# Expert weights of 64 tokens: five spread units on TensorE and 128 accumulating transfers by GpSimd in place of six units

## The reference, cut to what matters

```python
q = (hb @ w_q).reshape(n, PEER_HEADS, 2, PEER_HALF)            # 8 heads, 2 sides: 16 "sides" of 128
s = jnp.einsum('nhid,hikd->nhik', q, sub_keys)                 # 128 scores for each side
s_top, i_top = lax.top_k(s, PEER_TOPK)                         # 16 of 128 for each side
cand = s_top[:, :, 0, :, None] + s_top[:, :, 1, None, :]
best, pos = lax.top_k(cand.reshape(n, PEER_HEADS, 256), PEER_TOPK)
idx = take_along_axis(cand_idx, pos)                           # one of 16384 experts = 128 x 128
w = jax.nn.softmax(best, axis=-1)
act = jax.nn.gelu(einsum('nhkd,nd->nhk', u_tab[idx], hb))
out = einsum('nhk,nhkd->nd', w * act, v_tab[idx])
```

## Time and profile before

| | |
|---|---|
| median of 3 runs | 2785.63 us |
| the profiled execution's own time | 2787.02 us |
| its span | 2785.2 us |
| TensorE busy | 2717.4 us |
| VectorE, ScalarE, GpSimd busy | 1929.9, 1030.8, 621.7 us |
| query stage | about 855 to 949 us |
| pass over U | about 953 to 1606 us |
| pass over V | about 1610 to 2130 us |

### The profile page before, as it was taken

How to read it: one execution, slowest core, us unless ns; L and a number is a source line. 1 busy time by engine, 2 the same in 40 slices (tenths; PEclk the granted TensorE clock), 3 DMA queues, 4 the chain that set the end, 5 groups by cost and what they waited for, 6 DMA issues and landing times. The chain is left out here.

```text
span 2785.2 us, 41401 instructions
## 1 busy us (share of the span) xinstructions
PE 2717.4 (98%) x15226; PEld 2352.7 (84%) x15226; DVE 1929.9 (69%) x3331; ACT 1030.8 (37%) x1505; POOL 621.7 (22%) x436
## 2 busy tenths in 40 slices
PE   8999999999999999999999999999999999999998
PEld 7887788898887898999999988888887777788887
DVE  7676563434545579999968778888888655588843
ACT  6433343223333343444444333333334434332222
POOL 4333100000000166566664322222220000100000
PEclk9999999999999999999999999999999999999999
DMA  3111222211223267899999999999996211223332
GB/s 131 46 54 54 76 96 79 82 39 61 94 96 106 91 198 260 252 292 293 292 285 353 363 323 345 346 346 348 343 345 216 64 51 61 68 99 99 99 89 78
DMA packets 254581, 488.27 MB, mean 175 GB/s; under 512 B 102737, under 2 KB 160209, under 8 KB 253666
## 3 DMA queue, kind: packets, MB, share of 16 engines
q1 hardware_dynamic: 199138, 326.88, 35.8%
q0 software_dynamic: 36864, 134.23, 13.2%
q10 hardware_dynamic: 18432, 25.17, 2.6%
HBM read 437.97 MB, written 48.23 MB: 175 GB/s over the span
## 5 line engine op out<-in xcount | busy, mean ns | idle before, releaser
L285 PE MATMUL banks<-weights_high,experts_third 128*128 128x512 f32 x768 | 298.8, 389 | 1.0 <-DVE experts_third L2335 1.0
L287 PE MATMUL banks<-weights_high,experts_third 128*128 128x512 f32 x768 | 298.8, 389 | 0.0
L286 PE MATMUL banks<-weights_low,experts_third 128*128 128x512 f32 x768 | 298.8, 389 | 0.0
L2146 POOL TENSOR_TENSOR weights_low<-weights_raw,weights_high 128x1024 fp32r<-128x1024 f32 x66 | 158.2, 2396 | 468.8 <-ACT weights_high L2045 468.6
L285 PE MATMUL banks<-hn_high,weights_high 128*128 128x264 f32 (+1 forms) x736 | 253.5, 344 | 4.4 <-DVEq L2698 1.7
L2102 ACT ACTIVATE weights_high<-weights_raw 128x1024 fp32r<-128x1024 f32 x128 | 135.8, 1061 | 328.7 <-PE banks L287 328.7
L285 PE MATMUL banks<-hb_high,weights_high 128*128 128x384 f32 x688 | 238.1, 346 | 9.2 <-POOL weights_low L2146 9.2
L286 PE MATMUL banks<-hn_low,weights_high 128*128 128x264 f32 (+1 forms) x736 | 246.8, 335 | 0.0
L287 PE MATMUL banks<-hn_high,weights_low 128*128 128x264 f32 (+1 forms) x736 | 245.6, 334 | 0.0
L287 PE MATMUL banks<-hb_high,weights_low 128*128 128x384 f32 x688 | 231.3, 336 | 0.0
L286 PE MATMUL banks<-hb_low,weights_high 128*128 128x384 f32 x688 | 231.2, 336 | 0.0
(11 more groups left out here) (579 smaller groups left out, 7084.3 us busy)
## 6 DMA issues: line engine op xcount, KB each, us to landing
weights_raw<-in_u SPq DMA_DIRECT2D x128, 512.0 KB, 3.4
weights_raw<-in_v SPq DMA_DIRECT2D x128, 512.0 KB
early_experts<-experts_A ACTq DMA_DIRECT2D x128, 192.0 KB
shared<-early_experts SPq DMA_DIRECT2D x128, 192.0 KB
weights_raw<-in_w_up SPq DMA_DIRECT2D x44, 512.0 KB, 3.4
expert_weights<-shared SPq DMA_DIRECT2D x40, 512.0 KB
shared<-expert_weights SPq DMA_DIRECT2D x128, 160.0 KB
weights_raw<-in_w_xbc SPq DMA_DIRECT2D x24, 512.0 KB, 3.4
```

What stands on the lines that cost most here:

```text
L285: nc.tensor.matmul(to, w[0], x[0], start=start, stop=False)
L286: nc.tensor.matmul(to, w[0], x[1], start=False, stop=False)
L287: return nc.tensor.matmul(to, w[1], x[0], start=False, stop=stop)
L2146: nc.gpsimd.tensor_tensor(u_places[t % 3][1], raw[:, t % RING, :], u_places[t % 3][0].bitcast(F32), ALU.subtract).then_inc(u_low, 1)
```

## The change

- The first unit (tokens 128 to 191) isn't spread. Its 64 x 128 weights are added to the table in HBM by 128 indirect transfers of GpSimd, one per choice, each with 64 partitions and 4 bytes a partition, with add as the operation. Every 16 of them wait until the earlier ones have landed, since two heads may choose one expert. Their columns of the table are zeroed in the query stage by 8 stores of SP.
- Five units are spread, at the tiles of the new `SPREAD_AT`; block 1 has one unit, blocks 2 and 3 have two. Four are stored.
- Twelve of the 16 sides are scored by PE in the middle of query tiles 3 to 14 and copied back by ScalarE; of these VectorE ranks sides 0 to 11 of block 0 and 6 to 11 of block 1 in the query stage, 18 rows. The other four sides are scored before tile 0 for all blocks; the tables follow tile 0.
- Two `settle()` of `route_choice` take dots. `EXP_AT`, `DOT_AT` and `GATHER_AT` are some 3 or 4 tiles earlier. Low parts go to VectorE from tile 96 on instead of 100.

```diff
+RANKED_EARLY = (tuple(range(0, 12)), tuple(range(6, 12)), (), ())
+SIDES_EARLY = 12
-EXP_AT = (13, 27, 50, 76)
-SPREAD_AT = [start + min(i // 3, 4) for start in (30, 42, 56, 68, 83, 95) for i in range(HALF // PER)]
+EXP_AT = (10, 24, 45, 71)
+SCATTERED = HALF
+FIRST_SPREAD = 1
+SPREAD_AT = [start + at for start in (27, 52, 64, 79, 91) for at, n in enumerate((3, 3, 3, 3, 4)) for i in range(n)]
+SCATTER_AT = [t for t in range(28, 126) for _ in range(2 if t > 95 else 2 if t in SPREAD_AT else t % 2)]
+SCATTER_AT = SCATTER_AT[:P]
+ZERO_PARTS = 8
...
 GATHER_AT = (
-    39, 41, 42, 43, 44, 44, 44, 45, 45, 45, 46, 46, 47, 52, 53, 54, 56, 57, 58, 58, 58, 59, 59, 59,
+    37, 39, 40, 41, 42, 42, 42, 43, 43, 43, 43, 43, 44, 49, 49, 50, 52, 53, 54, 54, 54, 55, 55, 55,
...
# queries_phase, SP
+                    if m - RING < ZERO_PARTS:
+                        sp.dma_start(w_dram[(m - RING) * rows:(m - RING + 1) * rows, :, 0:SCATTERED].rearrange("i j n -> j i n"),
+                                     zeros[:].unsqueeze(1).to_broadcast([P, rows, SCATTERED])).then_inc(zeroed, 16)
...
+                sp.wait_ge(zeroed, 16 * ZERO_PARTS)
# queries_phase, PE
+                def score(r):
+                    if r == 0:
+                        pe.wait_ge(*keys_loaded)
+                    pe.wait_ge(evicted, r + 1)
+                    if r >= 2:
+                        pe.wait_ge(scores_out, r - 1)
+                    for b in range(NB):
+                        last = nc.tensor.matmul(B[:, SCORES + r % 2, b * P:(b + 1) * P], q[:, b, r, :], keys[:, r, :], start=True, stop=True)
+                    last.then_inc(scored, 1)
...
+                        if c == 3 and 0 <= m - 3 < SIDES_EARLY:
+                            score(m - 3)
# queries_phase, VectorE, once for each of the five ranking steps, around evict, normed and hb_low
+                    for b in rows:
+                        rank(nc.vector.max(top[b][:, r, 0:8], q[:, b, r, :]))
                     evict(m - 2)
+                    ranked()
...
# experts_phase, SP before the pass over V
-                sp.wait_ge(w_stored, 16 * STORES * (HALVES - 1))
+                sp.wait_ge(w_stored, 16 * STORES * (SPREAD_HALVES - 1))
+                sp.wait_ge(scattered, 16 * P)
# experts_phase, GpSimd
+                def scatter(g):
+                    if g == 0:
+                        pool.wait_ge(row_index, 7)
+                    elif g % TOPK == 0:
+                        pool.wait_ge(scattered, 16 * g)
+                    nc.gpsimd.indirect_dma_start(table, bass.IndirectOffsetOnAxis(ap=place[0:SCATTERED, g:g + 1], axis=0),
+                                                 place_w[0:SCATTERED, g:g + 1], None, compute_op=ALU.add).then_inc(scattered, 16)
...
+                    for n in scatters_after(t):
+                        scatter(n)
                     for g in gathers_after(t):
# experts_phase, VectorE after route_choice(1)
+                    if b == 1:
+                        settle()
+                        nc.vector.scalar_tensor_tensor(row_f[:], picked[:, 0, :], float(KEYS), picked[:, 1, :], ALU.mult, ALU.add
+                                                       ).then_inc(row_index, 1)
+                        nc.vector.tensor_copy(place_w[:], picked[:, 2, :]).then_inc(row_index, 1)
+                        dve.wait_ge(row_index, 6)
+                        nc.vector.tensor_scalar(place[:], row_f[:], float(STORED), column[:, 0:1], ALU.mult, ALU.add).then_inc(row_index, 1)
                     dve.wait_ge(chosen_out, b)
```

More of the change, by code:

```diff
@@ L1579, in _ @@
                 add_skip(G - 1, NB - 1)
[L1582 removed]
+RANKED_EARLY = (tuple(range(0, 12)), tuple(range(6, 12)), (), ())
+SIDES_EARLY = 12
+EARLY_STEPS = 5 * sum(len(r) for r in RANKED_EARLY)
+ROWS_LEFT = [[r for r in range(2 * PEER_HEADS) if r not in early] for early in RANKED_EARLY]
+STEPS_TO = [EARLY_STEPS + sum(5 * (len(ROWS_LEFT[i]) + PEER_HEADS) + 25 for i in range(b)) for b in range(NB + 1)]
 HALF = 64
 PER = 4
+LOW = -3.0e38
 DENSE = SEQ - P
 STORED = DENSE - HALF
[L1587 to L1588 removed]
+EXP_AT = (10, 24, 45, 71)
[5 more added lines that the diff above has]
+ZERO_PARTS = 8
 TAIL = SPREAD_AT[-1] + 1
@@ L1643, in _ @@
             def _(sp):
+                sp.wait_ge(constants_set, 1)
                 for m in range(RING, TILES):
@@ L1762, in _ @@
                         k.split_low(dve)
+                    r = m - 5
+                    rows = [b for b in range(NB) if r in RANKED_EARLY[b]]
+                    if rows:
+                        dve.wait_ge(scores_out, r + 1)
+                    for b in rows:
+                        rank(nc.vector.max(top[b][:, r, 0:8], q[:, b, r, :]))
                     evict(m - 2)
+                    ranked()
+                    for b in rows:
+                        rank(nc.vector.max_index(idx[b][:, r, 0:8], top[b][:, r, 0:8], q[:, b, r, :]))
                     if 4 <= m < 4 + KD:
@@ L1767, in _ @@
                                                        ).then_inc(scaled, 1)
+                    ranked()
+                    for b in rows:
+                        rank(nc.vector.match_replace(q[:, b, r, :], top[b][:, r, 0:8], q[:, b, r, :], LOW))
                     if 6 <= m < 6 + KD:
@@ L1773, in _ @@
                                                 ).then_inc(hb_low, 1)
+                    ranked()
+                    for b in rows:
+                        rank(nc.vector.max(top[b][:, r, 8:16], q[:, b, r, :]))
+                    ranked()
+                    for b in rows:
+                        rank(nc.vector.max_index(idx[b][:, r, 8:16], top[b][:, r, 8:16], q[:, b, r, :]))
+                assert done[0] == EARLY_STEPS
 def begin_load_phase(k, name, pairs):
@@ L1789, in gathers_after, with scatters_after @@
     return [g for g in range(P) if GATHER_AT[g] == t]
+def scatters_after(t):
+    return [n for n in range(len(SCATTER_AT)) if SCATTER_AT[n] == t]
 def slot_uses(g):
@@ L1799, in spread_groups, with spread_from, experts_phase @@
     return [n for n in range(len(SPREAD_AT)) if SPREAD_AT[n] == t]
+def spread_from(b):
+    return max(0, 2 * (b - 1) - FIRST_SPREAD) * (HALF // PER)
 def block_begun(t):
     groups = spread_groups(t)
-    return groups[0] // (HALF // PER * 2) + 1 if groups and groups[0] % (HALF // PER * 2) == 0 else 0
-def experts_phase(k, name, following, q, out, keys, hb, u, v, u_rows, by_token, gathered, early, w_dram, ws, es, keys_loaded):
+    return {spread_from(b): b for b in range(1, NB)}.get(groups[0], 0) if groups else 0
+def experts_phase(k, name, following, q, out, keys, hb, u, v, u_rows, by_token, gathered, early, w_dram, ws, es, ranks, tops, idxs):
     nc = k.nc
@@ L1895, in _ @@
                         sp.dma_start(raw[:, t % RING, :], u[t]).then_inc(raw_in[t % RING], 16)
-                    for half in range(HALVES - 1):
+                    for half in range(SPREAD_HALVES - 1):
                         last = SPREAD_AT[(half + 1) * GROUPS - 1]
@@ L1927, in _, with score_rest @@
             def _(pe):
-                def score(b):
-                    if b:
-                        pe.wait_ge(scores_out, b)
-                    for r in range(SIDES):
-                        last = nc.tensor.matmul(B[:, 2 + r // 4, (r % 4) * KEYS:(r % 4 + 1) * KEYS], q[:, b, r, :],
-                                                keys[:, r, :], start=True, stop=True)
+                def score_rest():
+                    for r in range(SIDES_EARLY, SIDES):
+                        for b in range(NB):
+                            last = nc.tensor.matmul(B[:, 2 + r - SIDES_EARLY, b * P:(b + 1) * P], q[:, b, r, :], keys[:, r, :],
+                                                    start=True, stop=True)
                     last.then_inc(scored, 1)
@@ L2274, in one_hots @@
                         dve.wait_ge(spread_done, n - 1)
-                    four = slice(n * PER, (n + 1) * PER)
-                    here = (n * PER) % P
+                    four = slice(column_of(n), column_of(n) + PER)
+                    here = column_of(n) % P
                     pairs = [P, 2, PER, P]
@@ L2291, in _ @@
                 nc.vector.tensor_copy(row_i[:], row_f[:]).then_inc(row_index, 1)
+                nc.vector.tensor_tensor_reduce(below, k.const("ident"), k.const("iota"), 1.0, 0.0, ALU.mult, ALU.add, column[:, 0:1]
+                                               ).then_inc(row_index, 1)
                 for b in range(1, NB):
-                    start = SPREAD_AT[(b - 1) * 2 * GROUPS]
+                    first, end = spread_from(b), spread_from(b + 1)
+                    start = SPREAD_AT[first]
                     dots_to = sum(at < start for at in DOT_AT)
@@ L2307, in _ @@
                         one_hots(n)
+                    if b == 1:
+                        route_scores(b + 1, sum(d < start + 12 for d in DOT_AT))
                 for t in range(TAIL, TILES):
@@ L4034, in first_experts @@
```

(3 more changed lines are left out.)

130 lines of the change are left out of this document (75 added, 55 removed), and 22 rows, old and new, of tables (DOT_AT, GATHER_AT).

## The result

| | before | after |
|---|---|---|
| median (6 runs each) | 2785.67 us | 2856.77 us (2854.26 to 2868.24) |
| ratio, 95% interval | | 1.0264 [1.0249, 1.0278] |
| span of the profiled execution | 2785.2 us | 2855.0 us |
| GpSimd busy | 621.7 us | 807.9 us |

The change costs 71 us. The forecast was 2766, in a range of 2750 to 2800: wrong in size and in sign. Rival A (GpSimd becomes the bound) had the right kind.

What follows compares the result with a forecast made beforehand. The prediction took TensorE, busy in 98% of the span, as the bound. Terms -14.4 + 0.5 - 8.3 - 4.8 + 4 + 3 = -20.0 us took the profiled 2787.0 to 2767.0, as median 2766 us; range 2750 to 2800.

Steps and rivals of the forecast that it cites:

- Rival A: GpSimd becomes the bound in the tail if a scatter costs 2 us or more, deciding from 1.35: about 2822; chance 0.12.
- Five units: Pass over U: five spread units in place of six remove 16 groups of 0.90 us from TensorE, -14.4 us.
- Scores and ranking in the query stage: Scores of 12 sides and 18 ranking rows move into the query stage: price 0.5 us, bounds 0 and 5.
- Zeroing: Query stage: zeroing 4 MB by 8 stores on SP's queue is hidden, price 0; one late tile, 2 us, if uncovered.
- steps 4 to 6: Stops in the pass over U: earlier routing -8.3, other planned places -4.8, burst of gathers +4 us.
- Step 4: Earlier routing, with dots in two self-waits, shrinks the stop around tile 28 from 10.3 to 2 us: -8.3.
- no 6 us wait of TensorE before tile 28: A sign the forecast held: TensorE's stop before tile 28, 5.85 us in the earlier trace, would be gone.
- Step 6: Gathers bunched in tiles 42 and 43 make tile 44 wait: +4 us, bounds 0 and 8.
- step 7: The 128 scatters on GpSimd, taken at 1.0 us each, mostly fit its free time: +3 us, bounds 0 and 40.
- 108 us of 121 available: Tiles 96 to 124: 58 scatters and 40 gathers fill GpSimd for 108 of 121 us, plus three 4 us waits.
- All three signs: Signs against the forecast: scatter pitch over 1.3 us, VectorE waiting for rows in the tail, new low-part waits over 12 us.
- Rival B: The transfers themselves are slow, loading the full DMA engines in the tail by 38 us: 2804; chance 0.09.

Runs made afterwards that it cites:

- e1: The changed kernel without its 128 scatters and the waits for them, weights of tokens 128 to 191 left out: 2769.87 us, ratio 0.9942 to the kernel before.
- e4: The kernel before with one edit, the two bare self-waits in route_choice carrying dots: 2786.18 us, ratio 1.001.
- e5: The changed kernel with six spread units and the kernel before's tile tables, no scatters, place arithmetic or zeroing, early scores and ranking kept: 2783.40 us, 0.9994.
- e3: The changed kernel with scatters of four kinds: unchanged, 32 partitions, 16 partitions, and 64 without add; some weights lost: 2836.78 us, one execution.
- e8: The changed kernel with all 128 scatters as plain writes without the add, part of the weights lost: 2816.66 us, ratio 1.0106 to the kernel before.
- e10: The changed kernel with two choices a transfer, 64 transfers of 128 partitions in new places (42 before tile 96, 22 after), nothing left out: 2776.56 us, 0.9968.
- e7: The changed kernel with a dummy GpSimd multiply of 128 x 800 elements in place of each scatter, those weights left out: 2839.65 us, ratio 1.0196.
- e12: The kernel of e10 with gathers and transfers laid out anew by a count of GpSimd's time per tile: 2783.75 us, ratio 0.9995 to the kernel before.

## Why the prediction was wrong, step by step

1. **Five units.** Right: 640 records in place of 768.
2. **Scores and ranking in the query stage.** Right: the stage is 10.9 us longer, of which 10.7 are the moved scores themselves (48 matmuls at 0.22 us, from a tile of 7.74 us with 16 of them in place of 4.16), so 0.2 us net at 0.5 forecast. The row indices come 44.2 us after the first Gelu in place of 66.6, 22.4 nearer; forecast 23.
3. **Zeroing.** Right: no late tile, and the last weights came in time.
4. **The stops (steps 4 to 6).** -8.3 - 4.8 + 4 = -9.1 forecast, some -2 measured (e1 2769.9, where the steps give 2763). Step 4 is where the trace was misread: e4 and e5 show that neither the dots in the self-waits nor the early ranking moves the stop by itself. In e1 tile 26 still lasts 11.66 us in place of 4.16. In the changed kernel's own trace it lasts 4.49 us, and the forecast's sign "no 6 us wait of TensorE before tile 28" came; the last section shows that this varies with the execution. Whether the stop shows is chance in part. Step 6, the burst of gathers, was put at 4 and costs 7.2 us at tiles 43 and 44.
5. **The scatters (step 7): the step that failed,** "I take 1.0" and "Price +3". A scatter measured 1.49 + 0.26 us, and 128 of them cost 86.9 us. Two terms were wrong. The price: the add was taken as free and the partitions as what counts, and e3 shows the reverse. The room: e8 paid 1.25 and still lost 46.8 us. Before tile 96 I had written "8.2 us at worst against 6.86 for two tiles running, within a reserve of 5 us", but the units have two or three such tiles; at 1.74 a scatter they are 9.6 us against 6.86, 2.7 a tile. And "108 us of 121 available" in the tail left no room to fetch a row ahead of its dot, where the trace showed a lead of 14.2 us. All three signs that the prediction named for being wrong came: a pitch of 1.74 us (over 1.3), VectorE waiting for rows in the tail (81.1 us), and TensorE's waits for low parts (33.0 us before tile 96 and 35.1 behind, over 12).

Rival A's mechanism is what happened. Its deciding price of 1.35 us was too high: e8 loses at 1.25. (That price also leaves out the 8 us of reserve that its sum for 2 us takes off; with them the tail would cost 11 us at 1.35, not 20.) Its 2822, worked out for 2 us a scatter, fell short of what 1.74 did, because it left the places before tile 96 at 10 us where they cost 32. In the tail its sum falls short too. At 1.74 us, 58 scatters with 40 gathers and 12 us of landing make 163 us for 121, less 8 of reserve 34; measured are 49.8, with stops and a lower clock that GpSimd's time alone doesn't count.

**Rival B, slow transfers, was wrong.** The median from issue to landing of the gathers is 5.5 to 5.7 us in the changed kernel and 6.2 to 6.5 in e1; the share of the DMA engines falls behind tile 95, from 0.95 to 0.83. The Trainium skill, "DMA: Bandwidth & Descriptors", section "Rules for kernel authors" (coalesce small transfers), pointed to the right side: e10 against the changed kernel agrees with it, 80 us less with 64 transfers in place of 128, though they are newly placed too. But what is paid here is the issuing engine's time. Its section "Anatomy of one DMA" (about 2.0 us fixed a transfer) would by an estimate have made seven landing waits 14 us. Three were found, 7.2 us in all and up to 3.3 each, in the changed kernel, and four in e10, 12.0 us in all and up to 4.1 each: fewer waits, but longer ones than 2.0 us.

What stays open: 5 us between e7 and the changed kernel, how much of e7's cost came through VectorE, and what part of e10's gain is the halving and what part the new places.

## What to carry to other kernels

Before work is moved from the bound engine to an idle-looking one, write for each tile what the receiving engine has to do and what time the tile gives, with measured pitches: GpSimd was busy for 22% of the span and still had no room, since its free time lay elsewhere: from 1083 to 1606 us of the pass over U it was busy for 287.2 of 523 us, 55%. An operation that no trace shows (here the accumulate) is measured by one small run or carried at the price of its worst neighbour, and its range gets the full price. When one engine's transfers have a price that hardly depends on their size, first halve their number and spread them, which here paid together.

## What the runs showed of the hardware

- **An indirect transfer holds GpSimd for a time that hardly depends on its partitions, and an add is dear.** 0.93 us for a plain one of 64 partitions; with add 1.31, 1.33, 1.43 and 1.59 us for 16, 32, 64 and 128 partitions, medians; and 0.30 us to the next.
- **A low part on GpSimd shuts out small operations of VectorE, and a low part on VectorE holds up GpSimd's transfers.** e1 and the changed kernel are the same up to tile 27, and yet the turn of block 1 came 7 us later in e1. Of VectorE's timeline, the same operation in e1 and then in the changed kernel:

```profile
1051.91 3.05 DVE L2330 TENSOR_SCALAR experts_wide<-experts_partsf 128x128 f32<-128x128 f32 x1
```

```profile
1052.24 0.23 DVE L2333 TENSOR_SCALAR experts_wide<-experts_partsf 128x128 f32<-128x128 f32 x1
```

  In e1 a gather of GpSimd runs up to 1052.43 and a low part from 1052.44 to 1054.86, and VectorE's operation ends at 1054.96; in the changed kernel the operation falls between two transfers, with no low part running. Three such meetings (2.2, 1.7 and 2.8 us) make the 7 us. Before the first of them VectorE was half a microsecond apart in the two traces (70.20 and 69.66 us after the first matmul of the pass), so a small difference in phase becomes one of several us at the turn. Of the ten traces with this routing, Gelu to Gelu, tile 26 takes 4.5 us in two (the changed kernel and e12), 7.0 to 8.4 in three, and 11.5 to 11.9 in five. The 2.94 us of the earlier trace rows was one: it ends 0.09 us behind a low part of GpSimd. The other way round, two transfers of GpSimd in the tail of the changed kernel, and the operations of VectorE under which they begin, are:

```profile
1579.97 2.46 POOL L2230 DMA_INDIRECT expert_weights<-experts_place_w,experts_place  x1 [0.30 <-issue]
...
1587.03 2.14 POOL L2230 DMA_INDIRECT expert_weights<-experts_place_w,experts_place  x1 [0.30 <-issue]
```

```profile
1579.88 1.22 DVE L2420 TENSOR_TENSOR weights_low<-weights_raw,weights_high 128x1024 fp32r<-128x1024 f32 x1
...
1586.60 1.22 DVE L2420 TENSOR_TENSOR experts_third<-weights_raw,experts_third 128x1024 fp32r<-128x1024 f32 x1
```

  with 1.03 and 0.71 us over the usual 1.43, where 1.13 and 0.79 us of VectorE's operation were left. Ten of the 58 scatters of the tail take 1.65 to 2.46 us, and each of these begins under a low part of VectorE with 0.3 us or more of it left. The other 48, and the 70 before tile 96, where GpSimd makes the low parts, take 1.47 at most. The Trainium skill, "SBUF — State Buffer", section "SBUF: two separate sides", has this as an exclusive lock on a port pair that the two engines share; for VectorE's operations under a low part the traces agree. For transfers that section names the case of VectorE in a two-port mode. Here it is a subtraction of two SBUF operands, and the transfers wait all the same.
